# Experts' weights in six slots instead of four

## The reference, cut to what matters

```
grp_prob = softmax(t @ w_route_group + b_route_group)      # 4 groups, each token takes 1
p_grp, g_sel = top_k(grp_prob, 1)
p_exp, e_sel = top_k(softmax(exp_logits of that group), 2) # 4 experts a group, 2 taken
for e in range(16):
    he = silu(t @ w_e_gate[e]) * (t @ w_e_up[e])           # 2048 -> 512
    y = y + combine[:, e:e+1] * (he @ w_e_down[e])         # 512 -> 2048
```

## Time and profile before

| | us |
|---|---|
| median of 3 runs (lowest, highest) | 3308.83 (3307.78, 3310.36) |
| the profiled execution | 3304.67 |
| its span, first to last instruction | 3302.9 |
| PE busy in the span | 3166.9 (96%) |
| DVE busy | 1857.9 (56%) |
| ACT busy | 1396.1 (42%) |

### The profile page before, as it was taken

The page is one execution under the profiler, slowest core; times in us unless marked ns, Lnnn a source line. Parts: engine busy times, 40 slices in busy tenths (PEclk is TensorE's granted clock), DMA queues, the critical chain, the costliest instruction groups (busy, mean ns, idle before and its releaser), DMA issues.

```text
span 3302.9 us, 46085 instructions
## 1 busy us (share of the span) xinstructions
PE 3166.9 (96%) x18702; PEld 2718.0 (82%) x18702; DVE 1857.9 (56%) x2416; ACT 1396.1 (42%) x1951; POOL 211.2 (6%) x263
## 2 busy tenths in 40 slices
PE   8999999998989999999898899999999999999998
PEld 7777777766768888767797779999998989889896
DVE  3433333356577777767656883444565555545454
ACT  2222222244456666656541013665434434434343
POOL 0000000020000000000137630000000000000000
PEclk9999999998989999999999998999999999999999
DMA  6222222221358888778553333444555555555554
GB/s 239 83 77 77 90 77 79 88 77 67 115 210 325 318 324 315 286 284 308 190 190 119 124 114 123 166 164 178 208 191 179 204 191 185 186 189 183 189 184 148
DMA packets 81782, 581.66 MB, mean 176 GB/s; under 512 B 9009, under 2 KB 9265, under 8 KB 12338
## 3 DMA queue, kind: packets, MB, share of 16 engines
q1 hardware_dynamic: 78912, 566.27, 47.3%
q10 hardware_dynamic: 2674, 12.54, 1.0%
HBM read 574.58 MB, written 4.19 MB: 175 GB/s over the span
## 4 chain that ended last, share of the span: by engine, by line
PE 80%; DVE 11%; DMA 3%; ACT 2%; POOL 2%; issue 1%; SPq 0%; ACTq 0%; DVEq 0%; POOLq 0%
PE PG L784 10%; PE PG L724 8%; PE PG L722 8%; PE PG L725 8%; PE PG L750 5%; PE PG L749 5%; PE PG L748 5%; PE PG L1103 3%; PE PG L1104 3%; PE PG L1105 3%; PE PX L854 3%; DMA ring<-weights 3%; DVE work L2344 2%; DVE ring_r L612 2%; PE PG L693 1%
## 5 line engine op out<-in xcount | busy, mean ns | idle before, releaser
L612 DVE TENSOR_TENSOR ring_r<-ring,work_r 128x1024 fp32r<-128x1024 f32 x532 | 629.9, 1225 | 394.7 <-ACT work_r L605 389.7
L605 ACT ACTIVATE work_r<-ring 128x1024 fp32r<-128x1024 f32 x532 | 534.4, 1052 | 577.5 <-PE PG L725 235.1
L784 PE MATMUL PG<-HT,ring 128*128 128x256 f32 x1728 | 435.1, 389 | 0.0
L612 DVE TENSOR_TENSOR ring_r<-ring,C_r 128x1024 fp32r<-128x1024 f32 x244 | 289.2, 1226 | 222.2 <-ACT C_r L605 218.9
L605 ACT ACTIVATE C_r<-ring 128x1024 fp32r<-128x1024 f32 x244 | 244.9, 1052 | 374.7 <-PE PG L725 255.6
L725 PE MATMUL PG<-work_r,ring_r 128*128 128x256 f32 x1344 | 374.8, 279 | 0.0
L725 PE MATMUL PG<-YT_r,ring_r 128*128 128x256 f32 x1280 | 361.2, 282 | 0.0
L784 PEld LDWEIGHTS PG<-HT,ring 128*128 128x128 f32 x1728 | 311.2, 190 | 55.4 <-issue 10.6
L725 PEld LDWEIGHTS PG<-work_r,ring_r 128*128 128x128 f32 x1344 | 253.3, 188 | 0.0
L749 PE MATMUL PG<-ring_r,HT_r 128*128 128x512 f32 x640 | 252.1, 394 | 0.0
L725 PEld LDWEIGHTS PG<-YT_r,ring_r 128*128 128x128 f32 x1280 | 244.5, 191 | 0.0
(11 more groups left out here) (566 smaller groups left out, 6277.0 us busy)
## 6 DMA issues: line engine op xcount, KB each, us to landing
ring<-weights SPq DMA_DIRECT2D x536, 1024.0 KB, 4.8
XT<-xT SPq DMA_DIRECT2D x4, 512.0 KB, 6.1
XT<-x ACTq DMA_DIRECT2D x1, 2048.0 KB, 9.4
residual<-XT ACTq DMA_DIRECT2D x4, 512.0 KB, 3.0
XT<-residual ACTq DMA_DIRECT2D x1, 2048.0 KB, 10.1
result<-YT SPq DMA_DIRECT2D x8, 256.0 KB, 4.1
C<-constants ACTq DMA_DIRECT2D x1, 1608.0 KB, 9.3
work<-gate_up ACTq DMA_DIRECT2D x1, 1024.0 KB, 13.0
```

Source lines behind the costliest of these rows:

```text
L605: act.activation(w_high(u)[:, c], ring[:, u % RING, c], ACT.Copy).then_inc(w_hi, 1)
L612: dve.tensor_tensor(ring_r[:, u % RING, c], ring[:, u % RING, c], w_high(u)[:, c].bitcast(F32), ALU.subtract).then_inc(w_lo, 1)
L784: mm = pe.matmul(PG[:, u % BANKS, 0:T], ring[:, u % RING, k * P:k * P + P], HT[:, k, :], start=(k == 0), stop=(k == KT - 1))
```

## The change

In the experts' stage the units rotate over six slots in place of four: the four of `ring` (0 to 3), slot 4 in `C[:, 0:2048]`, and slot 5 in the last 2048 columns of the gathered tokens' tile, the low half of the smallest group's slots. `slot(u)` gives the slot, `loads(u)` how many loads that slot has had. Outside the stage the ring of four is as before. `MOE_SLOTS = (4, 5, 0, 1, 2, 3)`, so the first two loads need no wait on PE, and the last four places lie in slots 0 to 3, as the second block expects. From place 6 on a load waits for the unit six before it; places 2 to 5 keep the wait of a ring of four. `FOLD` moves from `C` to `SQ`. Two semaphores that nothing used go, and two `slot_full` come. No instruction of PE, ACT or DVE is added or taken away: only the tile differs that they name for a unit. Two waits of SP go.

```diff
+MOE_SLOTS = (4, 5, 0, 1, 2, 3)
+def slot(u):
+    return MOE_SLOTS[(u - U0["moe"]) % len(MOE_SLOTS)] if U0["moe"] <= u < U0["p2"] else u % RING
+def loads(u):
+    n = u - U0["moe"]
+    if n < 0:
+        return u // RING + 1
+    if u < U0["p2"]:
+        return n // len(MOE_SLOTS) + 1 + (U0["moe"] // RING if slot(u) < RING else 0)
+    moe = U0["p2"] - U0["moe"]
+    return u // RING + 1 - moe // RING + moe // len(MOE_SLOTS)
...
-        slot_full = [sem(f"slot_full{i}") for i in range(RING)]
+        slot_full = [sem(f"slot_full{i}") for i in range(len(MOE_SLOTS))]
...
-        FOLD = C[0:HALF, 0:512]
+        FOLD = SQ[0:HALF, 0:2, :].rearrange("p a t -> p (a t)")
...
+        def weights(u):
+            return (ring[:, slot(u), :] if slot(u) < RING else C[:, 0:UNIT] if slot(u) == RING else
+                    work[:, (2 + LAST) * PIECE - UNIT:(2 + LAST) * PIECE])
+        def w_low(u):
+            return (ring_r[:, slot(u), :] if slot(u) < RING else C_r[:, 0:UNIT] if slot(u) == RING else
+                    slots(LAST - 1, 1))
...
-            act.wait_ge(slot_full[u % RING], 16 * (u // RING + 1) + more * 4)
+            act.wait_ge(slot_full[slot(u)], 16 * loads(u) + more * 4)
...
-                sp.wait_ge(unit_done, u + 1 - RING)
-                sp.dma_start(ring[:, u % RING, :], A["weights"][bass.ds(at, 1), :, :].rearrange("o p n -> p (o n)")) \
-                  .then_inc(slot_full[u % RING], 16)
+                if n > 1:
+                    sp.wait_ge(unit_done, u + 1 - (RING if n < len(MOE_SLOTS) else len(MOE_SLOTS)))
+                sp.dma_start(weights(u), A["weights"][bass.ds(at, 1), :, :].rearrange("o p n -> p (o n)")) \
+                  .then_inc(slot_full[slot(u)], 16)
```

More of the change, by code:

```diff
@@ L362, in build @@
             sem("root_ready"), sem("normed_tiles")
-        s_sqsum = sem("squares_summed_over_partitions")
         s_mixed = sem("prev_scaled")
@@ L397, in build @@
         pool_chain = sem("pool_chain")
-        c_pow = sem("s5_powers")
         g_in, g_sq, g_sum, g_ms, g_rt, g_vn, g_t, g_tt, g_mix, g_y = (sem("gmlp_" + n) for n in (
@@ L604, in split_high @@
                 c = slice(h * UNIT // 2, (h + 1) * UNIT // 2)
-                act.activation(w_high(u)[:, c], ring[:, u % RING, c], ACT.Copy).then_inc(w_hi, 1)
+                act.activation(w_high(u)[:, c], weights(u)[:, c], ACT.Copy).then_inc(w_hi, 1)
         def split_low(dve, u, more=0):
@@ L611, in split_low @@
                 dve.wait_ge(w_hi, 2 * split_count(u) + h + 1 + more * 2)
-                dve.tensor_tensor(ring_r[:, u % RING, c], ring[:, u % RING, c], w_high(u)[:, c].bitcast(F32),
+                dve.tensor_tensor(w_low(u)[:, c], weights(u)[:, c], w_high(u)[:, c].bitcast(F32),
                                   ALU.subtract).then_inc(w_lo, 1)
@@ L684, in unit @@
             def unit(u, use, x, kts=KT, tiles=1, first=None, full=0, free=0):
-                pe.wait_ge(slot_full[u % RING], 16 * (u // RING + 1) + full)
+                pe.wait_ge(slot_full[slot(u)], 16 * loads(u) + full)
                 for t in range(tiles):
@@ L720, in split_unit @@
                             c = slice((k * tiles + t_) * P, (k * tiles + t_) * P + P)
-                            wh, wl = w_high(u)[:, c], ring_r[:, u % RING, c]
+                            wh, wl = w_high(u)[:, c], w_low(u)[:, c]
                             pe.matmul(o, wh, high[:, k, :], start=(n == 0 and not (down and t_ % 2)), stop=False,
@@ L741, in tokens_unit @@
                         before(k)
-                    wh, wl = w_high(u)[:, kk * 512:kk * 512 + 512], ring_r[:, u % RING, kk * 512:kk * 512 + 512]
+                    wh, wl = w_high(u)[:, kk * 512:kk * 512 + 512], w_low(u)[:, kk * 512:kk * 512 + 512]
                     for tt in range(TT):
@@ L1139, in expert_out @@
                         pe.wait_ge(w_lo, 2 * split_count(u) + 2)
-                    wh, wl = w_high(u)[:, k * 512:k * 512 + 512], ring_r[:, u % RING, k * 512:k * 512 + 512]
+                    wh, wl = w_high(u)[:, k * 512:k * 512 + 512], w_low(u)[:, k * 512:k * 512 + 512]
                     for i in range(expert_tiles(r)):
```

## The result

| | before | changed | ratio (95% interval) |
|---|---|---|---|
| median, first session (4 and 4 runs) | 3309.6 | 3280.8 (3278.0 to 3285.4) | 0.9912 (0.9895 to 0.9929) |
| median, second session (17 and 5 runs) | 3303.9 | 3280.2 (3278.1 to 3282.6) | 0.9925 (0.9912 to 0.9939) |
| profiled execution, first session | 3304.67 | 3280.27 | |

The change saves 24 to 29 us; the two profiled executions stand 24.4 us apart. I had forecast 14 us and a range that ended at 3283. The way was right and the size too small. The kernel before spreads over 3298 to 3314 us in the two sessions, which is why the medians of the first session stand 28.8 us apart and those of the second 23.7.

The account below looks back on a forecast made before the run. PE fills most of the chain; from 1300 to 1620 us late loads reach it through ACT and DVE. 4.1 + 7.0 + 1.0 + 2.5 - 0.6 = 14.0 us off 3308.83 gives a median of 3294.8, range 3283 to 3307.

Parts of the forecast that it names:

- four short units: Places 180 to 183 ask for a split every 1.8 us, DVE needs 2.27 us each; no slot helps there.
- the two turns: PE's two long stalls, 4.07 and 4.80 us (8.9 us), behind late loads and DVE's work: 4.1 us comes back.
- PE waits for the split itself: 11 stalls from 1300 to 1620 us, 10.0 us, with only ACT's and DVE's first piece behind the load: 7.0 us back.
- sums of outputs: PE waits of 3.5 + 0.5 us in DVE's backlog of 1565 to 1590, behind the load of 1558.56: 1.0 us back.
- clock: PE's granted clock of 0.98 from 1300 to 1620 us: 5 us counted as real loss, half, 2.5 us, comes back.
- places: Split and PE use two slots in other tiles, 4 ns a matmul: 0.6 us slower, at most 3.6 us either side.
- Loads were behind all of it: Rival: with loads early every PE stall from 1300 to 1620 us goes, with the clock: 27.9 us, 3281; chance 0.08.
- DVE's order is the wall: Rival: three high tiles and program order hold DVE; only a third of 10.0 us comes back, 3305.5; chance 0.19.
- optimize those engines that are blocking the critical path: Cited under the rival of DVE's order: the blocker is DVE, not transfers; by that alone no gain, 3309.
- Loads in flight share the engines: Rival: six loads out divide the DMA engines, the needed one lands 6.1 us late three times: 18.3 us slower, 3327; chance 0.06.
- 358 GB/s: HBM to SBUF rate by a skill page, against 426 traced: slots fill at under half the pace, median 3302; set aside.

Follow-up runs that it names:

- the turn before the split: Changed kernel, but at places 114 and 149 DVE makes the turned tile's low half before the split of two units on: 3278.47 us, ratio 0.9921.

## Why the prediction was wrong in size

The step that failed is how the sum turned late loads into PE's loss. It took that loss to be the idle time that the views show, which put 4.1 to 4.4 us between marks 2 and 3 and all 1.5 between 1 and 2 at nothing; and of the idle time it held back 3 us at four short units, where 2.7 came back. That late loads were the cause was right. Step by step, by the parts of the sum. The measured numbers are of the profiled executions.

| term | forecast | measured |
|---|---|---|
| the two turns | 4.1 | 8.9 - 4.4 = 4.5 |
| PE waits for the split itself | 7.0 | 10.0 - 0.3 = 9.7 |
| sums of outputs | 1.0 | 4.0 - 3.3 = 0.7 |
| clock | 2.5 | 0.9 and 2.4 (two profiles) |
| places | -0.6 | none |
| part of the waits that no idle time shows | 0 | 4.1 to 4.4 |
| marks 1 to 2 | 0 | 1.5 |
| before mark 1, after mark 3 | 0 | 3 or less, differs by execution |

**The reading of the views was right in the main.** ACT's waits for loads went from 87.6 to 1.4 us (forecast: under 20) and turned into waits for PE's units; the two turns kept a stall each of 2.4 and 2.0 us (forecast: about 2.5); idle time fell to 8.0 us (forecast: about 11); DMA's rate rose to 296 GB/s (forecast: about 293). DVE's order was shown to be the wall at the turns, for 2.2 of 4.4 us. Two waits for the sums of outputs, 1.7 and 1.6 us in the kernel before (1577.56 and 1585.40 us), did not come from the load of 1558.56, as I had argued: they are 1.7 and 1.6 us in the changed kernel, and 1.6 to 2.1 in each version with whole loads. The 0.7 us that did go were two smaller waits. What holds the two was not tested.

**The term that was mis-sized.** "Stalls in which PE waits for the split itself" had 3 us held back for the four short units at places 180 to 183, of which I said that no slot helps there. It was wrong. By place, PE waited 0.38, 0.49 and 1.32 us before places 182, 183 and 184, and of these 2.2 us only 0.32, before place 184, are left. DVE needs 2.27 us a unit and PE asks for one each 1.8 us, but over four units that is only 4 x 0.5 = 2 us, and with loads in time DVE can come to them with two splits in hand; that is an argument, which no run took apart. I took DVE's backlog of 1565 to 1590 for a fixed sum of work, while much of it was work pushed together by the late load of 1558.56: it went with the lateness alone, in the kernel that waits five back as well.

**The term that was missing.** I took PE's loss for its idle time. But a matmul is shown for 0.39 us and the next could start 0.23 us after it began. Three rows of the kernel before, at one stall:

```profile
1507.15 0.39 PE L1096 MATMUL PG<-ring_r,work_tokens 128*64 128x512 f32 x1
1508.67 0.50 PE L1155 MATMUL PG<-work_r,YT_r 128*128 128x512 f32 x1 [1.14 <-DVE ring_r L612]
1509.01 0.39 PE L1156 MATMUL PG<-ring_r,YT_r 128*128 128x512 f32 x1
```

From start to start are 1.52 us, of which 0.23 are due: the loss is 1.29 us, not 1.14. Each of the 17 waits hides 0.15 us so, and 12 of them went: 1.8 us. Waits shorter than that show no idle time at all. Counting starts that follow one another after 0.27 to 0.40 us between marks 2 and 3, the kernel before has 41 with 4.1 us more than 0.23 each, and the changed kernel 17 and 20 with 1.5 and 1.8: 2.3 to 2.6 us, in which a part of the clock's steps is counted too. Of the 1.5 us between marks 1 and 2, 0.6 are two waits that are shown (0.17 and 0.41 us), 0.3 lie hidden in these, 0.5 are too short to be shown, and 0.1 is spread over all steps. There the window had PE busy 357.59 of 360 us, and I read "transfers cost nothing there". I had said that PE's busy time has overlap in it, and did not draw the conclusion.

**The clock.** By windows of 2 us, (1 - granted clock) x PE's busy time between marks 2 and 3 comes to 5.7 us before, 4.8 and 3.3 in the changed kernel, and 1.6 with the turn before the split. The two other kernels that wait four back in this stretch gave 7.7 and 6.1, so this term is known to some 2 us only. After the second stall it stood at 0.50 from 1452 to 1456 us; in the changed kernel the windows at the same stall, which ended at 1438.72, have this:

```profile
1436.00:1440.00 4.00, 2.02 (x12) 1.51 (x10) 4.00 (x5) 3.10 (x5) 0.00 (x0) 0.93 0.90 328
1440.00:1444.00 4.00, 4.00 (x13) 3.20 (x12) 1.44 (x2) 0.00 (x0) 0.00 (x0) 0.65 0.49 207
```

In the second profile of the changed kernel it did not fall after that stall; these are the end of the stall and the 4 us behind it:

```profile
1440.00:1444.00 4.00, 2.02 (x11) 1.54 (x9) 4.00 (x6) 2.92 (x4) 0.00 (x0) 1.00 0.95 373
1444.00:1448.00 4.00, 4.00 (x19) 3.21 (x18) 1.04 (x1) 0.00 (x0) 0.00 (x0) 1.00 0.31 131
```

So it fell after the stall of 2.4 us in both profiles, after that of 2.0 us in one of them, and after neither of the two stalls (1.2 and 1.1 us) with the turn first. In all of these it fell once more after the two waits of 1.7 and 1.6 us for the sums. My half, 2.5 us, is at the upper end of what was measured.

**The sum** for marks 2 to 3: 14.9 us of waits shown, 1.8 hidden in them, 2.3 to 2.6 too short to be shown, and 0.9 or 2.4 of clock make 20.2 and 21.4; measured 20.0 and 21.4. With 1.5 and 1.4 us between marks 1 and 2 that is 21.5 and 22.8 us. The rest to 24 us lies before mark 1 and after mark 3 and differs from run to run. Against the forecast of 14.0 the first profile is 10.4 us more: 4.2 by what no idle time shows, 2.7 by the waits for the split, 1.5 between marks 1 and 2, 1.0 by the turns and the places, 2.9 outside the marks, less 0.3 for the sums and 1.6 for the clock.

**The rivals.** "Loads were behind all of it" gave 3281 and came nearest, at a chance of 0.08; its mechanism was overstated, since 8.0 us of waits and most of the clock's loss stay. That its number fits is luck: the waits that it did not know of stand in for those that stayed. "DVE's order is the wall" fell: ACT's waits and PE's both went. The rule "optimize those engines that are blocking the critical path", which I cited from the Trainium skill ("Perfetto Trace Analysis", Optimizing DMA Performance), read as "DVE, since each PE wait names it", would have kept the kernel as it was; the engine named as releaser was itself held by a load two steps back. "Loads in flight share the engines" did not come, but the changed kernel hardly asked for it: from place 111 on four loads were out at once a single time, and otherwise at most three, as before. The median landing from 1300 to 1560 us is 6.0 to 6.1 us by slot, against 5.7 before. What speaks against the rival is the start of the stage with six loads out: they landed one after another, and not all near 17 us. The 358 GB/s of the Trainium skill's page "SBUF — State Buffer" did not bind either: the window at 948 us above has 430 GB/s, and from 1300 us on the mean of 296 lies under both figures, so the runs do not show what such a bound would have cost.

## What to carry to other kernels

Where a pipe has several stages, look one stage further than the releaser that the wait names: a wait for DVE, behind ACT, behind a load, is a wait for the load. Compare a load's landing time with the time of the units between its release and its use. Late loads cost only where the units behind them are too short to hide them: here ACT waited 98.9 us for loads from 960 to 1300 us, which cost some 1.5 us, and 87.6 us after that, which cost 20. One slot more was enough, and gave what two gave. And count an engine's loss from start to start of its instructions, where the profile draws them longer than their spacing.

## What the runs showed of the hardware

Where the moving weights lie did not matter to PE. In the changed kernel line 1130 has medians of 392, 394 and 389 ns for a matmul of 512 columns from the ring, the constants and the tokens' tile, and line 1182 has 392 to 393, 389, and 392 to 396: the order turns round, and all lie within 8 ns.

Loads of 1 MB from one queue landed one after another: alone 4.8 us after issue, and with six issued within 3.2 us up to 15.2 us, 2.5 us from one landing to the next. From place 111 on the median is 4.8 us alone, 5.6 with one other still out and 6.8 with two in the kernel before, and 4.8, 5.3 and 7.1 in the changed one.

The granted clock differs between executions of one program: the same twelve matmuls before mark 1 started 0.23 us apart in one profile of the changed kernel and 0.43 in the other.
